# Who issues the query loads in a latent-attention loop: SyncE between its transposes, or GpSimd

## What is computed

```python
def dsa_attention(q, k_lat, q_idx, k_idx, w_idx):
    # which keys each query keeps is decided by an indexer beforehand
    k_sel  = k_lat[top_idx]
    logits = einsum('bqhd,bqkd->bqhk', q, k_sel) * scale
    p      = softmax(where(valid, logits, -inf))
    ctx    = einsum('bqhk,bqkc->bqhc', p, k_sel[..., 64:])
# then ctx @ w_uv per head, @ w_o, and LN(alpha*x + mixer(x))
```

## Time and profile before

| | us |
|---|---|
| median of 3 runs | 2828.64 (2826.52 to 2830.71) |
| profiled execution, its own time | 2825.56 |
| its span in the trace | 2823.8 |
| PE busy (share of the span) | 2678.5 (95%) |
| DVE busy | 1901.3 (67%) |
| ACT busy | 1087.2 (39%) |
| POOL busy | 1667.5 (59%) |
| the attention stage | about 1795 to 2090 |

### The profile page before, as it was taken

How to read it: one execution, slowest core, us unless ns; L and a number is a source line. 1 busy time by engine, 2 the same in 40 slices (tenths; PEclk the granted TensorE clock), 3 DMA queues, 4 the chain that set the end, 5 groups by cost and what they waited for, 6 DMA issues and landing times.

```text
span 2823.8 us, 42342 instructions
## 1 busy us (share of the span) xinstructions
PE 2678.5 (95%) x15765; PEld 1358.4 (48%) x16048; DVE 1901.3 (67%) x2637; ACT 1087.2 (39%) x1665; POOL 1667.5 (59%) x916
## 2 busy tenths in 40 slices
PE   7999888899999999999899999888899999999998
PEld 4566554354444444444444444455554444444443
DVE  6788778575666674255999999788847656664043
ACT  3566566243333210014554333677743433331000
POOL 4777656336776679845348777700013666675884
PEclk9999999999999999999999999999999999999999
DMA  4122456631111253333213222499983111113332
GB/s 150 50 64 72 91 119 119 192 116 60 54 53 59 68 179 127 100 133 84 54 38 141 109 77 104 116 195 195 196 223 126 68 60 60 60 55 126 126 105 97
DMA packets 312623, 297.98 MB, mean 106 GB/s; under 512 B 252721, under 2 KB 252849, under 8 KB 312481
## 3 DMA queue, kind: packets, MB, share of 16 engines
q1 hardware_dynamic: 300672, 272.05, 34.2%
q10 hardware_dynamic: 11808, 23.99, 2.6%
HBM read 189.51 MB, written 35.70 MB: 80 GB/s over the span
## 4 chain that ended last, share of the span: by engine, by line
PE 77%; DVE 6%; DMA 6%; issue 4%; ACT 3%; POOL 2%; ACTq 1%; POOLq 0%; SPq 0%; DVEq 0%
PE ps L1691 23%; PE ps L334 19%; PE ps L316 14%; DMA pt<-split 5%; PE ps L650 4%; PE ps L399 4%; PE ps L2513 3%; PE ps L2019 2%; PE ps L920 2%; PE ps L656 1%; PE ps L2063 1%; DVE split L848 1%; PE ps L891 1%; PE ps L2530 1%; DVE prob L1035 1%
## 5 line engine op out<-in xcount | busy, mean ns | idle before, releaser
L273 POOL TENSOR_TENSOR w_hi<-w_stage,ones 128x1024 bf16<-128x1024 f32 (+1 forms) x115 | 237.0, 2061 | 137.9 <-PE ps L334 85.3
L276 POOL TENSOR_TENSOR w_lo<-w_stage,w_hi 128x1024 bf16<-128x1024 f32 (+1 forms) x115 | 267.2, 2324 | 9.0
L1508 DVE SCALAR_TENSOR_TENSOR x_res<-x_res,ps 128x1024 f32<-128x1024 f32 x32 | 39.0, 1217 | 319.8 <-PE ps L334 318.9
L334 PE MATMUL ps<-w_hi,hid_hi 128*128 128x512 bf16 x689 | 206.1, 379 | 1.6 <-POOL w_lo L276 0.8
L334 PE MATMUL ps<-w_hi,hid_lo 128*128 128x512 bf16 x690 | 206.4, 379 | 0.7
L334 PE MATMUL ps<-w_lo,hid_hi 128*128 128x512 bf16 x690 | 206.4, 379 | 0.7
L2513 PE MATMUL ps<-lat_hi,q_now 128*128 128x512 bf16 (+3 forms) x729 | 185.9, 325 | 5.1 <-DVE row_max L2578 3.8
L316 PE MATMUL ps<-xt_hi,w_hi 128*128 128x512 bf16 x598 | 178.7, 379 | 3.1 <-DVE score L2178 2.5
L316 PE MATMUL ps<-xt_hi,w_lo 128*128 128x512 bf16 x596 | 178.2, 379 | 0.6
L316 PE MATMUL ps<-xt_lo,w_hi 128*128 128x512 bf16 x592 | 177.4, 379 | 0.8
L1691 PE MATMUL ps<-xt_lo,w_hi 128*128 128x512 bf16 x426 | 161.5, 379 | 0.5
(11 more groups left out here) (305 smaller groups left out, 7490.8 us busy)
## 6 DMA issues: line engine op xcount, KB each, us to landing
w_stage<-in_l_up SPq DMA_DIRECT2D x88, 512.0 KB, 3.8
w_stage<-in_l_down SPq DMA_DIRECT2D x88, 512.0 KB, 3.7
w_stage<-in_l_o SPq DMA_DIRECT2D x32, 512.0 KB, 6.0
w_stage<-in_l_q SPq DMA_DIRECT2D x32, 512.0 KB, 5.2
q_split<-q_out SPq DMA_DIRECT2D x32, 512.0 KB, 2.6
q_now<-q_split SPq DMA_DIRECT2D x16, 1024.0 KB, 5.8
w_stage<-in_l_qkv SPq DMA_DIRECT2D x24, 512.0 KB, 4.2
x_spilled<-x_res ACTq DMA_DIRECT2D x16, 512.0 KB, 2.6
```

The source lines that it names most:

```text
L273: pool.tensor_tensor(hi, w_stage[slot][:, 0:cols], ones[:, 0:1].to_broadcast([P, cols]), ALU.mult).then_inc(w_cast[slot], 1)
L276: pool.tensor_tensor(lo, w_stage[slot][:, 0:cols], hi, ALU.subtract).then_inc(w_split[slot], 1)
L334: mm = pe.matmul(ps[:, bank + h, :], a[:, k, rows], w[:, h * HALF:(h + 1) * HALF], start=(k == first and m == 0), stop=(k == tiles - 1 and ...
```

## The change

GpSimd issues the 14 loads of the pairs 1 to 7 in its own queue, with a semaphore of its own for each buffer (`s_qp`). SyncE's loop then holds only transposes. GpSimd's loop over the pairs is written out, so that the addresses are constants. Its order in each half is: wait for `t_qk`, issue the load, wait for `t_pv`, copy the values. TensorE waits on `s_q7` for pair 0 and on `s_qp` for the others. Before all that, GpSimd waits until the queries of all heads are stored in DRAM (`s_qst`), as SyncE does already.

```diff
+        s_qp = [sem(f"q_next_loaded{h}") for h in range(2)]
...
                     if t % 8 == 0:
-                        pe.wait_ge(s_q7[hh], 16 * (pair + 1))
+                        if prev is None:
+                            pe.wait_ge(s_q7[hh], 16)
+                        else:
+                            pe.wait_ge(s_qp[hh], 16 * pair)
...
         def attend_sync(sp):
-            def load_q(h, pair):
-                sp.dma_start(q_now[h][:, :, :, :],
-                             q_dram[bass.ds(4 * pair + 2 * h, 2)].rearrange("s p l t -> p s l t")
-                             ).then_inc(s_q7[h], 16)
...
                 for t in range(STEPS):
-                    if t in (6, 14) and pair + 1 < N_PAIRS:
-                        h = t // 8
-                        sp.wait_ge(t_qk, STEPS * pair + 8 * (h + 1))
-                        load_q(h, pair + 1)
                     turn(pair, t)
...
+            def load_q(h, pair):
+                pool.wait_ge(t_qk, STEPS * (pair - 1) + 8 * (h + 1))
+                pool.dma_start(q_now[h][:, :, :, :],
+                               q_dram[4 * pair + 2 * h:4 * pair + 2 * h + 2].rearrange("s p l t -> p s l t")
+                               ).then_inc(s_qp[h], 16)
+
             pool.wait_ge(s_vl, VAL_CHUNKS)
             for hh in range(2):
                 values_now(hh, 0)
+            for r in range(4):
+                pool.wait_ge(s_qst[r], 16 * feed_q.iters)
             split_first(pool, feed_o1)
-            with pool.Fori(1, N_PAIRS) as pair:
+            for pair in range(1, N_PAIRS):
                 for hh in range(2):
+                    load_q(hh, pair)
                     pool.wait_ge(t_pv, STEPS * (pair - 1) + 8 * (hh + 1))
                     values_now(hh, pair)
```

## The result

The changed kernel takes **2866.82 us** (median of 4 runs, 2861.26 to 2870.26) against 2827.58 us of the kernel before on the same chip (2826.31 to 2830.71): ratio 1.0136, 95% interval 1.0124 to 1.0148, **39 us slower**. The forecast was 2828, the range 2823 to 2846; both missed. The profiled execution took 2868.33 us with a span of 2866.5.

The account below looks back on a forecast made before the run. The prediction took the loop of VectorE, ScalarE and TensorE's scores as the bound, with no DMA in it. Terms: -0.6 for late transposes, +0.3 for the first load, -0.3 on 2828.64, given as 2828 us; range 2823 to 2846.

Parts of the forecast that it names:

- The loop VectorE, ScalarE, scores sets the pace: In the profiled stage, a loop without DMA takes 17.39 us per half and bounds the kernel; the change leaves it.
- Rival (a): The transposes were the limit after all: all 28.2 us of waits for `pt` saved, 2800 us; chance 5%.
- At most 1.2 us to win: Lateness that transposes put on the loop, over 12 halves: at most 1.2 us can come back, 0.6 taken.
- the waits for `pt` beside the loop: TensorE's 28.2 us of waits for transposes lie in its slack beside the loop of VectorE, ScalarE and scores.
- (d): The load doesn't matter, late transposes have another cause: 2829 us, inside the forecast; chance 72% together with the forecast.
- GpSimd's issue is hidden: 14 load issues on GpSimd, 1.5 us each taken, hidden because its only other loop work is two copies per half.
- Its being early is worth 0, and it now runs beside the transposes of steps 4 and 5: The load starts at about 1922.5 to 1924 instead of 1926, is needed a pair later, and the engines' share has room.
- well under way when the load starts: Argument against rival (b): step 4's transpose is already far along when GpSimd's load starts.
- 1 to 2.5 us: Time taken from GpSimd's wait to the load's first data, putting its start at about 1922.5 to 1924.
- Rival (b): The load swamps the transposes of steps 4 and 5: 20 to 34 us slower, 2848 to 2862; chance 12%.
- The hope beside it: If queues take turns packet by packet, step 4's transpose loses little over 1 us, within the spare; sum stays 0.
- Rival (c): GpSimd's issues and VectorE's loop instructions get in each other's way: 14 x 1.13 = 16 us, 2844; chance 8%.

Follow-up runs that it names:

- the filler: The changed kernel with eight TensorE matmuls into an unused bank ahead of its wait for step 4's transpose: 2850.21 us against 2828.37 for the kernel before, ratio 1.0077.

## Why the prediction was wrong

- **The loop VectorE, ScalarE, scores sets the pace: right.** Without loads the time is the same, with the load one place earlier in SP's order the halves are 17.38 to 17.43 us. Rival (a), 2800 us, is dead.
- **At most 1.2 us to win, and the waits for `pt` beside the loop: right**, by the same two kernels. That also bears out (d) as a reading of the kernel before: the loads did not matter where they stood.
- **GpSimd's issue is hidden: right.** It takes 0.71 to 0.72 us (the first 0.89), less than the 1.5 taken, and the kernel with tiny loads is 3 to 5 us above the kernel before, at least part of which is the meeting of the copies told above.
- **"Its being early is worth 0, and it now runs beside the transposes of steps 4 and 5": this is the step that failed.** It cost 39 us. Three things in it were wrong. First, the order: the prediction had step 4 "well under way when the load starts". In fact GpSimd issued the load at 1919.20 and SP the transpose of step 4 at 1919.69, and the load's first packets started 0.9 us after that, before the transpose had moved any. The start-up itself, 1.4 us from issue to first data, lies in the "1 to 2.5 us" taken. Second, "beside": in six of 14 halves the two did not share the engines at all, in six they took turns packet by packet, and the load got 90% of the engines' time. The room in the mean DMA share (0.41 in one stretch of the earlier trace rows) says nothing of who is served first. Third, what is late next: TensorE's lost clock and ScalarE's wait for its buffer, told in the next point.
- **Rival (b) was the right mechanism, with 12%, and too small a price.** Its premise, a 4 KB piece of the load for each small piece of a transpose, is what six loads did, and six did worse. The hope beside it, that with turns taken step 4 loses little over 1 us, did not come true: its transpose landed some 3 us later than before. (b) decided at 1.8 us of delay and said 20 to 34 us, 2848 to 2862. The delay without the clock is some 18 us by the estimate above, a little under its 20 to 34; the 1.8 us itself is doubtful, since half a load should then have cost 11 us. What it left out is the granted clock, some 13 us, and the long half, some 8: TensorE's idle time of 2.28 us in a loop where it had hardly any was followed by 3.4 us at 0.50. It also left out ScalarE as the transposes' second consumer, which waits for its `split` buffer, 0.75 us in the half shown.
- **Rival (c) exists, but not in this kernel's loss and not from the issue.** In the changed kernel VectorE's lower parts of 896 take 1.09 us, as before. Where it occurs it costs 0.4 us in a half, only where the loop is on time and the copies fall on the lower part of 896.
- **The range** was cut at 2846 by giving (b) 12% and leaving it out. The rows could have moved that chance: a start-up stretch of 78 GB/s and DMA shares near 1 were in the earlier trace rows, and nothing showed that small packets are served during a load.

Open: why a transpose that had already begun alternates with the load and one that had not stands still; that goes by the order of starts in these 14 loads, and no experiment varied it alone. Why the half from 1875.4 ran as it did, and its part in the 17 us that the filler gave back. Why a wait of some 2 us is followed by a lower clock in some halves and not in others. And what the late issue in GpSimd's queue costs beyond the meeting with the copies.

## What to carry to other kernels

A bulk load that is issued earlier for no deadline is not free: ask which small transfer becomes due during the few us it fills the DMA engines, and let it go behind that one. Here one place in the order was worth 36 us, while another queue at the old time cost 2 to 6. That queues take turns does not help a small transfer if the turns are packets of very different sizes. If an engine is made to wait in a loop where it was busy throughout, add the time that its clock can be lower afterwards to the price, and look for all who wait for the late transfer, those who want a buffer back among them.

Before spending work on waits that a profile names, take away their supposed cause altogether in one experiment: the run without loads shows in one step that there is nothing to win. The best version tried is the smallest, the load ahead of step 5 in SP's own queue, 2826 us, which can't be told from the kernel before.

## What the runs showed of the hardware

- A 1 MB load and the transposes queued at the same time did not share the DMA engines for 3.5 us (1920.6 to 1924.1) when the load's packets started first, in GpSimd's queue and in ScalarE's hardware queue alike. About 1 us of that is the load's first packet on each engine (1920.6 to 1921.6), during which no other packet starts.
- Where the transpose's packets had started first, the two queues alternated one packet for one, 209 of 4 KB and 209 of 256 B in 2.5 us, with 90.1% and 9.6% of the engines' time.
- GpSimd's issue of a 1 MB load took 0.72 us; from issue to landing 6.1 us, where SP's takes 5.8.
- After 2.28 us of idle time TensorE's granted clock was 0.50 for 3.4 us, but after 2.31 us in another half of the same trace it stayed at 1.00; with the waits filled by matmuls it stayed at 1.00 from 1823 us to the stage's end. A half with a drop was about 1.7 us longer than one without.
